# One step order changed in three places of a hybrid-layer kernel: who stores the embedding tiles, and when two layer-norm sums are taken

## The reference, cut to what matters

```python
def second_block(x, p, ...):
    mix = fox_mixer(x, attn_w_in, attn_b_f, attn_w_out)      # causal attention, 16 heads, with a forget gate
    x = layer_norm(ALPHA * x + mix, ln_mix_g, ln_mix_b)      # first layer norm (n1 in the kernel)
    ffn = conv_ffn(x, ffn_w_up, ffn_conv_w, ffn_conv_b, ffn_w_down)
    x = layer_norm(ALPHA * x + ffn, ln_ffn_g, ln_ffn_b)      # second layer norm (n2)
    gate = sigmoid(x @ ple_w_gate + ple_b_gate)
    return x + gate * (p @ ple_w_proj)                       # p: 256 features per token
```

## Time and profile before

| | value |
|---|---|
| median of 3 runs | 2693.12 us |
| profiled execution, its own time | 2693.12 us |
| its span (first to last instruction) | 2691.3 us |
| mean granted TensorE clock | 0.991 of full |
| PE busy | 2586.6 us (96%) |
| DVE busy | 1418.6 us (53%) |
| POOL busy | 1327.3 us (49%) |
| ACT busy | 1057.7 us (39%) |

### The profile page before, as it was taken

The page is one execution under the profiler, slowest core; times in us unless marked ns, Lnnn a source line. Parts: engine busy times, 40 slices in busy tenths (PEclk is TensorE's granted clock), DMA queues, the critical chain, the costliest instruction groups (busy, mean ns, idle before and its releaser), DMA issues.

```text
span 2691.3 us, 37487 instructions
## 1 busy us (share of the span) xinstructions
PE 2586.6 (96%) x12094; PEld 2089.5 (78%) x12094; DVE 1418.6 (53%) x2044; ACT 1057.7 (39%) x1923; POOL 1327.3 (49%) x1100
## 2 busy tenths in 40 slices
PE   8999999999999989999999999899999999999989
PEld 5788888877777778888878888676778888787777
DVE  5455543135655565435555555636776656714445
ACT  4333331065545541116777777612433332401121
POOL 3788873331222124431111111456578787577766
PEclk9999999999999999999999999999999999999999
DMA  3222224311111014321111111222222222533333
GB/s 103 83 78 64 69 95 169 117 38 40 39 47 39 32 48 148 109 68 52 40 40 39 39 39 40 75 98 79 90 78 83 81 82 78 176 118 125 121 129 118
DMA packets 101630, 215.57 MB, mean 80 GB/s; under 512 B 11152, under 2 KB 11280, under 8 KB 101536
## 3 DMA queue, kind: packets, MB, share of 16 engines
q1 hardware_dynamic: 74432, 135.82, 16.1%
q10 hardware_dynamic: 27104, 78.56, 8.2%
HBM read 177.57 MB, written 36.77 MB: 80 GB/s over the span
## 4 chain that ended last, share of the span: by engine, by line
PE 77%; DVE 7%; ACT 6%; issue 5%; DMA 2%; POOL 2%; ACTq 0%; DVEq 0%; POOLq 0%; SPq 0%
PE bank L629 18%; PE bank L692 17%; PE bank L918 14%; PE flip L918 7%; PE pv L918 3%; PE flip L1079 3%; PE bank L1105 3%; PE pv L1079 3%; PE pv L863 2%; DMA raw<-in_w 2%; POOL wlo L533 1%; PE score L835 1%; PE flip L848 1%; POOL whi L531 1%; PE score L832 1%
## 5 line engine op out<-in xcount | busy, mean ns | idle before, releaser
L531 POOL TENSOR_SCALAR whi<-raw 128x512 fp32r<-128x512 f32 x350 | 258.6, 739 | 1211.6 <-PE bank L692 724.5
L533 POOL TENSOR_TENSOR wlo<-raw,whi 128x512 fp32r<-128x512 f32 x350 | 501.4, 1433 | 29.2
L629 PE MATMUL bank<-b_lo,whi 128*128 128x512 f32 x496 | 198.0, 399 | 2.3 <-DVE b_hi L2016 2.3
L629 PE MATMUL bank<-a_hi,whi 128*128 128x512 f32 x464 | 184.9, 399 | 3.4 <-POOL wlo L533 2.0
L692 PE MATMUL bank<-b_hi,whi 128*128 128x512 f32 x384 | 154.9, 403 | 5.6 <-DVE fk_lo_odd L2114 3.2
L546 POOL TENSOR_TENSOR wlo<-a,whi 128x512 fp32r<-128x512 f32 x102 | 148.2, 1453 | 15.3 <-ACT whi L1473 15.3
L629 PE MATMUL bank<-b_hi,whi 128*128 128x512 f32 x368 | 147.8, 402 | 8.1 <-DVE b_lo L1984 6.6
L692 PE MATMUL bank<-a_hi,whi 128*128 128x512 f32 x368 | 149.1, 405 | 6.3 <-DVE s_z L2061 5.1
L692 PE MATMUL bank<-b_hi,wlo 128*128 128x512 f32 x384 | 151.5, 395 | 0.0
L692 PE MATMUL bank<-b_lo,whi 128*128 128x512 f32 x384 | 151.2, 394 | 0.0
L692 PE MATMUL bank<-a_lo,whi 128*128 128x512 f32 x368 | 145.6, 396 | 0.0
(11 more groups left out here) (528 smaller groups left out, 7234.8 us busy)
## 6 DMA issues: line engine op xcount, KB each, us to landing
raw<-in_w SPq DMA_DIRECT2D x350, 256.0 KB, 2.6
a<-in_pairs SPq DMA_DIRECT2D x136, 256.0 KB, 2.6
h_scr<-up_y ACTq DMA_DIRECT2D x22, 512.0 KB, 2.6
fc<-c_scr ACTq DMA_DIRECT2D x16, 512.0 KB, 3.6
stage<-h_scr ACTq DMA_DIRECT2D x22, 256.0 KB, 3.4
a<-h_scr ACTq DMA_DIRECT2D x21, 256.0 KB, 3.4
y_scr<-up_y ACTq DMA_DIRECT2D x8, 512.0 KB, 2.6
t_scr<-y_room ACTq DMA_DIRECT2D x8, 512.0 KB, 2.9
```

Of the source, the lines that this page charges most:

```text
L531: nc.gpsimd.tensor_scalar(hi, src, 1.0, 1.0, ALU.mult, ALU.mult).then_inc(w_hi, 1)
L533: nc.gpsimd.tensor_tensor(lo, src, hi.bitcast(F32), ALU.subtract).then_inc(w_lo, 1)
L629: last = nc.tensor.matmul(psum_ap, ws[w][:, k, :], a[:, kt, hs(h)], start=(first and i == 0 and j == 0), stop=(final and i == n - 1 and j ...
```

## The change

Three places of the second block are changed.

1. **PLE parts.** The stores to `ple_scr` are issued by ACT instead of SP (SP's loop over the weight units loses its two interruptions). ACT issues both halves; for the odd parts it waits for DVE's copy first. The copies move within the step: `ple_out` now stands at the end of ACT's and DVE's step, by a new table `PLE_OUT` (part s-3 in step s up to 11, parts 9 and 10 in step 12, then s-2, and parts 14 and 15 behind the loop). TensorE's order of parts is unchanged. POOL's adds run from tile 0 to tile 7, and the first copies wait for all eight (`x_whole` at 8 instead of 1).
2. **First norm.** `square_sum` stands behind tile j = 4 of the second half, not j = 5; DVE sums squares before it subtracts the mean; the scaling is spread two tiles a step over j = 4 to 7 instead of 2, 3, 3 over j = 5 to 7.
3. **Tail.** `square_sum(n2, 1)` stands behind gate 1, not gate 3; ACT and DVE take gates 2, 3 and 4 out one place later relative to the scaling of the norm.

```diff
+PLE_OUT = {s: (s - 3,) if s < 12 else (9, 10) if s == 12 else (s - 2,) for s in range(3, NST)}
@@ SP
-            for m in range(4):
-                ple_store(m)
-            unit(U_FOUT + 1)
-            for m in range(4, KT):
-                ple_store(m)
-            with sp.Fori(U_FOUT + 2, U_DOWN) as u:
+            with sp.Fori(U_MIX + 1, U_DOWN) as u:
@@ POOL
-            for j in (KT - 1, *range(KT - 1)):
+            for j in range(KT):
                 nc.gpsimd.tensor_tensor(b_hi_f[:, j, :], b_hi[:, j, :].bitcast(F32), b_lo[:, j, :].bitcast(F32), ALU.add).then_inc(x_whole, 1)
@@ PE, second half of the output projection
-                elif j == 5:
+                elif j == 4:
                     square_sum(n1, 0, KT - 1)
@@ PE, tail
-            for i in range(1, 4):
-                gate_half(i)
+            gate_half(1)
             square_sum(n2, 1, 2 * (KT - 1))
-            for i in range(4, 2 * KT):
+            for i in range(2, 2 * KT):
@@ ACT, forget_hi(j)
-                act.wait_ge(x_whole, j + 2 if j < KT - 1 else 1)
+                act.wait_ge(x_whole, j + 1)
@@ ACT, ple_out(i)
+                room = b_lo_f[:, KT - 1, hs(h)]
                 if h == 0:
                     if m:
                         act.wait_ge(ple_stored[0], 16 * m)
                     else:
-                        act.wait_ge(x_whole, 1)
+                        act.wait_ge(x_whole, KT)
                     act.wait_ge(tile_done[0], T_PLE + m + 1)
+                    nc.scalar.activation(room, bank[0][:], ACT.Copy).then_inc(tile_out[0], 1)
+                act.wait_ge(tile_out[h], T_PLE + m + 1)
+                act.dma_start(ple_scr[m, :, hs(h)], room).then_inc(ple_stored[h], 16)
@@ ACT, step s of the last pair
-                    if not fills and s - 1 in PLE_LATE:
-                        ple_out(PLE_LATE[s - 1])
...
                         elif s < KT:
                             forget_hi(s - 1)
+                        for i in PLE_OUT.get(s, ()):
+                            ple_out(i)
@@ DVE, second half of the output projection
+                for k in range(max(2 * j - 2, 1), min(2 * j, KT)):
+                    square_add(n1, 0, k)
                 if j < 4:
                     for k in (2 * j, 2 * j + 1):
                         centre(n1, 0, k)
-                for k in range(max(2 * j - 2, 1), min(2 * j, KT)):
-                    square_add(n1, 0, k)
-                if j > 4:
-                    scaled_and_lo(n1, 0, b_hi, b_lo, C_LN1G, C_LN1B, ((0, 1), (2, 3, 4), (5, 6, 7))[j - 5])
+                else:
+                    scaled_and_lo(n1, 0, b_hi, b_lo, C_LN1G, C_LN1B, (2 * j - 8, 2 * j - 7))
@@ DVE, tail
-            for i in range(3):
-                gate_out(i)
+            gate_out(0)
+            gate_out(1)
             scaled_and_lo(n2, 1, None, None, C_LN2G, C_LN2B, range(0, 2))
+            gate_out(2)
+            scaled_and_lo(n2, 1, None, None, C_LN2G, C_LN2B, range(2, 5))
             gate_out(3)
-            scaled_and_lo(n2, 1, None, None, C_LN2G, C_LN2B, range(2, 5))
-            gate_out(4)
             scaled_and_lo(n2, 1, None, None, C_LN2G, C_LN2B, range(5, KT))
```

More of the change, by code:

```diff
@@ L1345, in ple_out @@
                     else:
-                        act.wait_ge(x_whole, 1)
+                        act.wait_ge(x_whole, KT)
                     act.wait_ge(tile_done[0], T_PLE + m + 1)
-                    nc.scalar.activation(b_lo_f[:, KT - 1, hs(0)], bank[0][:], ACT.Copy).then_inc(tile_out[0], 1)
+                    nc.scalar.activation(room, bank[0][:], ACT.Copy).then_inc(tile_out[0], 1)
+                act.wait_ge(tile_out[h], T_PLE + m + 1)
+                act.dma_start(ple_scr[m, :, hs(h)], room).then_inc(ple_stored[h], 16)
             def forget_pair(it, pp, fills):
@@ L1403, in forget_pair @@
                         high(n)
-                    if not fills:
-                        for i in PLE_EARLY.get(s, ()):
-                            ple_out(i)
                     if s + 2 < NST:
@@ L1418, in forget_pair @@
                         sums_in(*following, s // 15)
+                if not fills:
+                    ple_out(2 * KT - 2)
+                    ple_out(2 * KT - 1)
                 fold(NST - 1)
@@ L1943, in _ @@
                 if j in (1, 4, 7):
-                    i = 3 + j // 3
+                    i = 2 + j // 3
                     gate_out(i)
                     gate_store(i - 1)
-            for i in range(6, 2 * KT):
+            for i in range(5, 2 * KT):
                 gate_out(i)
@@ L2133, in ple_out @@
                     else:
-                        dve.wait_ge(x_whole, 1)
+                        dve.wait_ge(x_whole, KT)
                     dve.wait_ge(tile_done[1], T_PLE + m + 1)
@@ L2647, in gate_out @@
                 v.scalar_tensor_tensor(ple[h][j], ple[h][j], col(C_LN2B + j), z[:, j, hs(h)], ALU.add, ALU.add).then_inc(g_sum, 1)
-            for i in range(3):
-                gate_out(i)
+            gate_out(0)
+            gate_out(1)
             scaled_and_lo(n2, 1, None, None, C_LN2G, C_LN2B, range(0, 2))
+            gate_out(2)
+            scaled_and_lo(n2, 1, None, None, C_LN2G, C_LN2B, range(2, 5))
             gate_out(3)
-            scaled_and_lo(n2, 1, None, None, C_LN2G, C_LN2B, range(2, 5))
-            gate_out(4)
             scaled_and_lo(n2, 1, None, None, C_LN2G, C_LN2B, range(5, KT))
-            for i in range(5, 2 * KT):
+            for i in range(4, 2 * KT):
                 gate_out(i)
```

2 lines of the change are left out of this document (removed).

## The result

| | before | after |
|---|---|---|
| median | 2693.05 us (4 runs, 2691.43 to 2693.26) | 2742.24 us (4 runs, 2740.82 to 2743.45) |
| ratio | | 1.0183, 95% interval 1.0166 to 1.0201 |
| span of the profiled execution | 2691.3 us | 2740.1 us |
| mean granted TensorE clock | 0.991 | 0.982 |

The account below looks back on a forecast made before the run. TensorE, busy 96% of the span, was taken as the bound, so time could change only where it waits. 2693.1 + 35 (PLE parts) - 0.6 (first norm) - 1.7 (tail) = 2725.8, taken as 2726 us; range 2716 to 2740.

Parts of the forecast that it names:

- the ring: Last head pair: each PLE part needs the previous one copied out, so steps become serial; gaps 28.9 and 45.6 us.
- place 3: Tail: TensorE waits for the last sum, but later waits before gates 5 and 7 go; -1.7 us, between -3 and +3.
- place 2: First norm: TensorE waits 4.2 us, but the first half pass then finds its tiles ready; -0.6 us, between -2 and +2.
- The start: Last head pair: the first copy waits for all eight POOL adds, so PLE part 1 starts 10.2 us late.
- my gaps: Forecast times from one PLE part to the next in the last head pair: 28.9 us for steps 4 to 7, then 45.6.
- three such places beyond those counted ... give 2 more: PLE parts 3, 10 and 12: lower clock behind long waits, at 1.26 us a part, partly hidden; 2 us more.
- the lower clock through the whole stage: Rival: in the PLE stage TensorE's lower clock holds throughout; 20 us more than the forecast, 2746 us; chance 0.13.
- Stores and SP: PLE stores: freeing SP is worth nothing, and ACT's 16 DMA issues cost 0.
- my bound of 5: PLE stores: 5 us if each of eight issues behind ACT's own copies cost a whole copy with hand-over, 0.62.
- I get 0.5 us of room there: Tail: gate 6 waits for ACT's gate 4, behind all eight `norm_hi`, with 0.5 us to spare.
- Late start only: Rival: PLE part 1 starts late but the ring keeps its old pace; part 15 12 us late, 2703 us; chance 0.13.
- Not slower: Rival: the PLE stage costs nothing, its 14 gaps averaging 2.95 us each; 2690.8 us; chance 0.06.

Follow-up runs that it names:

- the run with filled waits: Changed kernel plus idle matmuls, never read, in TensorE's waits ahead of PLE parts; 2738.42 us against the changed kernel's 2742.24.
- with ACT's stores: Kernel before with PLE copies at the end of the step and stores issued by ACT, old start kept; 2731.46 us against 2692.94.
- with SP's: Kernel before with only the PLE copies moved to the end of the step, SP still storing, old start kept; 2734.17 us against 2692.94.
- place 2 alone: Kernel before with only the first-norm edits of the change; 2696.87 us against 2693.24.
- the start alone: Kernel before with only POOL's adds in order 0 to 7 and the first copies behind all eight; 2699.24 us against 2693.24.

## Why the prediction was right in direction and short in size

- **What was missing.** Of the 16 us between 2726 and 2742.24, the ring has 7.2 (76.5 forecast with its 2 us of clock, 83.7 measured), place 3 has 5.3 and place 2 3.1. Each is taken up below.
- **The start**: 10.2 us late forecast. Against POOL's first add, part 1 started at 14.13 before and 24.15 after: 10.0.
- **The ring, gap by gap.** The mechanism was right. Forecast from part 1 to 15: 74.5 us; measured 83.7 (1805.31 - 1721.63); before 51.5. From part 1 to 7 my gaps gave 38.7; the changed kernel took 46.65, and with the clock held up it took 38.6 (1763.91 - 1725.31). That these agree is partly luck, since my 38.7 held 2.9 of lower clock. One gap was too short by its list: from part 3 to 4 (step 6) I gave 6.5 and left out `values` (`pv`, 1.46 us between these parts in the chain after); it took 9.8, and 8.2 with the clock up. The first two gaps, which held the clock term, came out at 9.9 and 5.6 with the clock up, where I gave 10.9 and 6.3. The other three gaps agree within 0.1 (5.2, 6.2, 3.5), and from part 7 to 15 I gave 35.8 and 37.0 were measured.
- **The failed step of the ring: the lower clock.** "three such places beyond those counted ... give 2 more" is the term that was mis-sized. I had 2.9 us in the gaps and 2 more, 4.9 together; the same matmuls took 11.5 us longer. I had priced the clock at those parts that follow the longest waits, and took from the earlier trace rows that the stage recovers between them (1.00 in 1718 to 1722). In the changed kernel it does not: 0.73 over the whole stretch from part 1 to 7, and turns, `values` and scores between the parts are slow too. My rival, the lower clock through the whole stage, asked 20 us more than the 4.9; 6.6 more came, and the measured time lies between the two. (Its own terms, 14 x 1.26 and half of that again, less 2.9, make 23.6 and not 20.) In the Trainium skill, "TensorE: Matmul & The Clock Gate", section "What's actually happening", the clock follows how busy the array has been; the run with filled waits agrees (0.96 against 0.73).
- **Stores and SP**: 0 forecast, 0.5 measured at the step's end. That was luck of the place: ahead of `high` the same stores cost 7.4 us, by ACT's wait for DVE's copy, which my bound of 5 did not have as its cause. In the Trainium skill, "DMA: Bandwidth & Descriptors", section "Issuing engines are not separate DMA queues", issuing from several engines saves only the sequencer's time for the issue; here no such saving shows (stage 106.5 with ACT's stores, 105.9 with SP's).
- **Place 2**: -0.6 forecast, +3.6 measured (+2.5 to the mean). The wait was right (4.2, measured 4.3), and the half pass started at 1867.2 in place 2 alone, as forecast at 1867.8. But it did not find "them ready": 1/std gained only 0.2 us (82.7 behind the projection's start, before 82.9), as the average itself ran at the lower clock, and DVE's scalings had the additions of the late tile 5 among them. It ended at 1876.24 with its own wait of 2.5 us, not at 1873.4.
- **Place 3**: -1.7 forecast, +3.6 measured. The wait for the sum was right (8.5 named, 8.4 measured), and the waits before gates 5 and 7 did go. The step that failed is "gate 6, which waits for ACT's gate 4, now behind all eight `norm_hi`; I get 0.5 us of room there". The order was seen, the room was not there: gate 6 waited 3.17 us for that copy. The lower clock behind this wait and behind the sum makes most of the rest: 4.3 us over twelve gates (12.17 + 59.06 - 12 x 5.58) where 2.8 were put, and an average of 2.05 us where 0.86 was put.
- **Rivals.** Late start only: the start alone costs 6, not 12. Not slower: a gap averaged 6.0 us (83.7 / 14), not 2.95.

## What to carry to other kernels

Where two lists share one buffer, the place of the copy-out inside its engine's step decides whether the two steps overlap or add: every instruction ahead of it that depends on the consumer's last product is in the ring. Price a stage that turns from bound by TensorE to waiting with its matmuls at the clock that the rows show behind waits, for all of them and not only for the first. An average that is asked for earlier gains only if the copies that free TensorE's banks do not stand behind the work that the average releases. Where a profile names an engine for a wait, or none, look whether another engine's instruction ends right before the wait does.

## What the runs showed of the hardware

- The lower clock can be bought off: 34 unread 128x512 matmuls in 38.6 us raised the mean clock of a stretch that was 67% busy from 0.73 to 0.96 and shortened it by 8.0 us; 6.0 of them were lost again in the rest of the stage.
- The time from the start to the last pair, the same code in all, differed by up to 5.9 us from execution to execution, and the unedited stretch from the projection to gate 0 by up to 5.8 us, so that differences of 3 us are to be read by stage.
- TensorE started 0.1 us behind the end of the ACT copy that freed its bank, at every wait of over 1 us before a gate in 19 traces; the profile's releaser for these waits was POOL's split or none.
